# The last narrow piece of the light expert in one bank, and its next rows turned later

## What is computed

```python
def swiglu(x, w1, w3, w2):
    return (jax.nn.silu(x @ w1) * (x @ w3)) @ w2
```

## Time and profile before

| what | us |
|---|---|
| median of 3 runs (lowest to highest) | 1273.45 (1273.17 to 1274.38) |
| the profiled execution | 1273.87 |
| its span, first to last instruction | 1272.2 |
| PE busy | 1237.2 (97%) |
| DVE busy | 813.7 (64%) |
| ACT busy | 659.9 (52%) |
| mean granted PE clock | 0.992 |

### The profile page before, as it was taken

How to read it: one execution, slowest core, us unless ns; L and a number is a source line. 1 busy time by engine, 2 the same in 40 slices (tenths; PEclk the granted TensorE clock), 3 DMA queues, 4 the chain that set the end, 5 groups by cost and what they waited for, 6 DMA issues and landing times.

```text
span 1272.2 us, 15917 instructions
## 1 busy us (share of the span) xinstructions
PE 1237.2 (97%) x6263; PEld 935.3 (74%) x6263; DVE 813.7 (64%) x783; ACT 659.9 (52%) x683; POOL 87.3 (7%) x77
## 2 busy tenths in 40 slices
PE   9999999999999999999999989999979999799998
PEld 7878888888888888888776665566655666556886
DVE  6867756655456677689865655445554455555997
ACT  7577444444355674477754444434443444445774
POOL 0600001000004200020000000000000000000300
PEclk9999999999999999999999989999989999899999
DMA  9654549554545444479999999999999999999993
GB/s 376 275 198 135 177 167 371 193 199 167 197 154 210 174 158 166 166 275 404 351 362 420 421 380 382 403 407 421 421 369 380 423 420 422 383 384 423 420 421 148
DMA packets 56687, 391.91 MB, mean 308 GB/s; under 512 B 6720, under 2 KB 6720, under 8 KB 11584
## 3 DMA queue, kind: packets, MB, share of 16 engines
q1 hardware_dynamic: 53104, 374.84, 74.8%
q0 software_dynamic: 3360, 15.74, 3.2%
q10 hardware_dynamic: 144, 0.26, 0.1%
HBM read 384.78 MB, written 11.80 MB: 312 GB/s over the span
## 4 chain that ended last, share of the span: by engine, by line
PE 85%; DMA 5%; issue 4%; DVE 3%; ACT 1%; POOL 1%; SPq 1%; DVEq 0%; POOLq 0%; ACTq 0%
PE ps L574 23%; PE ps L575 21%; PE ps L576 21%; PE ps L1701 14%; DMA raw<-in_units 4%; PE ps L1245 3%; DVE wl L569 2%; DMA h<-in_x 1%; ACT wh L539 1%; POOL rst L712 1%; PE ps L1304 1%; DVE h L2323 0%; PE ps L1572 0%; PE ps L1618 0%; SPq L650 0%
## 5 line engine op out<-in xcount | busy, mean ns | idle before, releaser
L569 DVE TENSOR_TENSOR wl<-raw,wh 128x2048 fp32r<-128x2048 f32 x250 | 574.6, 2302 | 362.0 <-ACT wh L539 356.6
L539 ACT ACTIVATE wh<-raw 128x2048 fp32r<-128x2048 f32 x250 | 478.8, 1917 | 422.5 <-DMA raw<-in_units 262.8
L574 PE MATMUL ps<-wh,XT_h 128*128 128x512 f32 x944 | 379.9, 402 | 0.3 <-DVE wl L569 0.3
L575 PE MATMUL ps<-wl,XT_h 128*128 128x512 f32 x944 | 368.5, 390 | 0.0
L576 PE MATMUL ps<-wh,XT_l 128*128 128x512 f32 x944 | 368.5, 390 | 0.0
L574 PEld LDWEIGHTS ps<-wh,XT_h 128*128 128x128 f32 x944 | 177.3, 188 | 60.0 <-issue 23.5
L576 PEld LDWEIGHTS ps<-wh,XT_l 128*128 128x128 f32 x944 | 177.3, 188 | 37.9
L575 PEld LDWEIGHTS ps<-wl,XT_h 128*128 128x128 f32 x944 | 177.6, 188 | 33.1
L1701 PE MATMUL ps<-raw,few_X 128*64 128x256 f32 (+1 forms) x1152 | 133.5, 379 | 22.0 <-issue 20.1
L1701 PEld LDWEIGHTS ps<-raw,few_X 128*64 128x64 f32 x1152 | 79.0, 144 | 69.0 <-issue 39.2
L574 PE MATMUL ps<-wh,moe_gT_h 128*128 128x512 f32 x220 | 91.4, 415 | 0.2 <-DVE wl L557 0.2
(11 more groups left out here) (288 smaller groups left out, 1017.4 us busy)
## 6 DMA issues: line engine op xcount, KB each, us to landing
raw<-in_units SPq DMA_DIRECT2D x350, 1024.0 KB, 9.1
x_rows<-in_zeros POOLq DMA_DIRECT2D x8, 512.0 KB, 8.0
raw<-in_boot SPq DMA_DIRECT2D x5, 512.0 KB, 8.0
cols<-x_rows POOLq DMA_DIRECT2D x4, 512.0 KB, 9.2
y_rows<-xs POOLq DMA_DIRECT2D x4, 512.0 KB, 8.2
y_rows<-in_zeros POOLq DMA_DIRECT2D x6, 256.0 KB, 17.0
h<-in_x SPq DMA_DIRECT2D x1, 1024.0 KB, 13.0
rows<-in_rows SPq DMA_DIRECT2D x1, 896.0 KB, 16.9
```

What stands on the lines that cost most here:

```text
L539: nc.scalar.activation(wh[:, U.split_slot(j), :], raw[:, U.raw_slot(j), :], ACT.Copy).then_inc(hi_ready, 1)
L569: nc.vector.tensor_tensor(wl[:, s, :], raw[:, U.raw_slot(j), :], wh[:, s, :].bitcast(F32), ALU.subtract).then_inc(lo_ready, 1)
L574: nc.tensor.matmul(o, xh, bh, start=start, stop=False)
L575: nc.tensor.matmul(o, xh, bl, start=False, stop=False)
```

## The change

`few_places` gives the narrow piece two places in bank 2 (columns 0 to 127 for the gate product and 128 to 255 for the up product) and doesn't use bank 3. `few_gate_unit` computes both with one product per chunk and half, whose moving operand takes 128 columns of `w1` and 128 of `w3` (two runs, 256 columns apart). The wait for `g_ready` of the piece before is now only at k == 2, which the narrow piece doesn't have. The rows of p + 3 are turned after down step 6 and no longer after step 3, and in the expert in position 0 those of its second expert ahead of step 6 and no longer ahead of step 4. ACT copies them in steps 7 and 8.

```diff
         def few_places(p, s):
-            width = 256 if s < WIDE else 128
-            return ps[:, 2, 0:width], ps[:, 3, 0:width], width
+            if s < WIDE:
+                return ps[:, 2, 0:256], ps[:, 3, 0:256], 256
+            return ps[:, 2, 0:P], ps[:, 2, P:2 * P], P
...
-                    if u in (6, 7) and p + 3 < E:
-                        rows_hi(p + 3, u - 6)
+                    if u in (7, 8) and p + 3 < E:
+                        rows_hi(p + 3, u - 7)
...
-                    if u in (6, 7) and scatter is None:
-                        rows_hi(2, u - 6)
+                    if u in (7, 8) and scatter is None:
+                        rows_hi(2, u - 7)
...
-                    if u == 4 and scatter_at is None:
+                    if u == 6 and scatter_at is None:
                         rows_T(2)
...
-                if s > 0 and k == (2 if s < WIDE else 0):
+                if s > 0 and k == 2:
                     pe.wait_ge(g_ready, pieces_done(p, s - 1))
...
-                    for o, at in ((z1, 0), (z3, 256)) if s == WIDE else (((z1, z3)[k // 2], 0),):
-                        of = [w[:, a, at + half * width:at + (half + 1) * width] for half in range(2)]
-                        last = few_halves(o, few_X[:, c, :], of, c == 0, c == KC - 1)
+                    if s < WIDE:
+                        o, of = (z1, z3)[k // 2], [w[:, a, half * width:(half + 1) * width] for half in range(2)]
+                    else:
+                        o = ps[:, 2, 0:2 * P].rearrange("p (z n) -> p z n", z=2)
+                        by_matrix = w[:, a, :].rearrange("p (z h n) -> p z h n", z=2, h=2)
+                        of = [by_matrix[:, :, half] for half in range(2)]
+                    last = few_halves(o, few_X[:, c, :], of, c == 0, c == KC - 1)
...
-                    if u == 3 and p + 3 < E:
+                    if u == 6 and p + 3 < E:
                         rows_T(p + 3)
```

## The result

The changed kernel takes 1255.4 us in the median of 4 runs (1254.77 to 1259.13), beside 1273.74 for the kernel before on the same chip. The ratio is 0.9862, with a 95% interval of 0.9842 to 0.9882. The profiled execution took 1254.77 us, 19.1 less than the profiled one of before (forecast 21.1). The range held the median, and the forecast of 1252.3 was about 3 us too low.

A forecast was written before the change was run, and what follows sets the result against it. PE and transfers were taken as nearly even, with PE waiting for bank 3 and transfers then pausing. The gains 1.5 + 7.0 + 6.6 + 6.0 = 21.1 us gave a median of 1252.3 us, range 1247.5 to 1258.5.

The forecast's parts named there:

- The wait is for bank 3, behind a landing: Before light unit 20, PE waits for DVE's `few_up`, queued behind a landed unit's split; three waits, 20.1 us, go.
- The products themselves, 0: In the six narrow units, 16 longer products with a two-run operand take about 1.95 us per unit, gaining nothing.
- Earlier pairs gain what transfers gain, 7.0 and 6.6 us: In the first and second pair, unbroken transfers at 421 GB/s regain 7.0 and 6.6 us.
- rival A: In the down part, 384 GB/s is its own limit, so each pair gains only 3.0 us; 1263 us, chance 0.08.
- The new wait, 1.1 + 2.6 + 2.6: Before the turn in down step 0, PE waits for DVE's `lo`: 1.1, 2.6 and 2.6 us in the three pairs.
- the start of light unit 23: In the third pair, light unit 23 starts at 1115.14 from its own pair's gain, about 21 us earlier in all.
- the last pair's own gain: In the third pair, PE gains 6.0 us by light unit 23 and keeps it to the end.
- The expert in position 0, 1.5 us: In the expert in position 0, turning rows later removes 2.37 us of PE idle time; 1.5 us gained, between 0 and 2.4.
- The clock: At the new waits before down step 0's turn, 2.6 us lies nearer to 2.37 us, which kept the full clock.
- rival B: In down step 0, the new wait lowers the clock, costing about 4 us in all; 1256.5 us, chance 0.17.
- the expected sign of no stretch below 1 in the pairs: In the profile after, the granted clock has no window below 1 in the pairs.
- The turned rows in the pairs: In the pairs, turning rows after down step 6 removes two waits of about 2.5 us, with no separate gain counted.

The follow-up runs named there:

- e3: The changed kernel with the narrow piece's two products sharing bank 3 and unit 20 waiting for `few_up` of piece 4 as before; 1270.0 us, ratio 0.9964.
- e6: The kernel before with rows turned late and DVE's `up` and `few_up` of piece 4 ahead of the split of wide unit 21; 1254.87 us, ratio 0.9842.
- e2: The kernel before with only the turns of rows moved as in the change; 1269.39 us, ratio 0.9968.
- e4: The changed kernel with ACT's and DVE's narrow-piece work and piece 4's copies before the split of wide unit 23 in the pairs; 1253.36 us, ratio 0.9837.
- e8: The changed kernel with light units 3 to 20 of each pair loaded by half only, results not the reference's; 1242.12 us, ratio 0.9745.
- e7: The changed kernel with the turn in the expert in position 0 put back ahead of step 4; 1256.73 us, ratio 0.9855.
- a0: The changed kernel, unaltered, run again as reference for later experiments; 1256.45 us, ratio 0.9849.
- e1: The changed kernel with the turns of rows back at their old places, so the narrow piece's change alone; 1263.86 us, ratio 0.9913.
- e5: The changed kernel with light unit 20 computed twice in each pair, 1.95 us more PE work each; 1253.59 us, ratio 0.9830.

## Why the prediction was right, step by step

- *The wait is for bank 3, behind a landing:* right, shown by e3 (bank 3 kept, wait kept), e6 (bank 3 kept, `few_up` earlier) and the one named releaser in e2.
- *The products themselves, 0:* right, 1.95 us each in e3.
- *Earlier pairs gain what transfers gain, 7.0 and 6.6 us:* measured 61.69 - 54.67 = 7.0 and 61.23 - 54.62 = 6.6. The landing of wide unit 22 in the third pair agrees: it comes 15.1 us earlier, as 1.5 + 7.0 + 6.6 says. That transfers would stay near 421 GB/s through the down part was the doubtful step, and rival A is out.
- *The new wait, 1.1 + 2.6 + 2.6:* measured 0.54 + 2.80 + 3.09 = 6.4. Its cause was named rightly (e4, e8), and so was the start of light unit 23: 21.0 us earlier, beside 21.1 in the sum. Of these 15.1 were there at the landing of wide unit 22, so the last pair's own gain up to there is 5.9 (forecast 6.0).
- *The expert in position 0, 1.5 us:* the first pair begins at 646.32, where it began at 647.77, 1.45 less. By times at the end (e7) the term can't be confirmed.
- *The clock:* the mis-sized term. I took 2.6 us of wait to be nearer to 2.37 us, which had shown the full clock, and left the low clock to rival B with 0.17. It came in the first trace, where it costs 21.0 - 19.4 = 1.6 us, so the expected sign of no stretch below 1 in the pairs failed. It came after about half of such waits in the other traces (a0, e1, e6, e7), once even after 2.37 us. Where it is absent (e4, e5) the medians are 1253.4 and 1253.6, close to the forecast of 1252.3, though each of these kernels has another edit of its own. So forecast and rival B are both partly true: the mechanism of B, at about half its price (4 us). The last expert gives back another 0.3 us (106.84 us from light unit 32 to the end of the span, 106.56 before).
- *The turned rows in the pairs, "in the terms above already":* right for the sum, but it hid how much hangs on them. Left where they were, they would have made a second new wait of 2.9 us with a low clock in two pairs (e1), and taken back about 7 of the 18 us. The prediction should have priced the change without them.

## What to carry to other kernels

When PE and transfers are nearly even, price a removed wait by what the transfers regain (spacing of the splits that a landing released), and look for the next operation that stands in an in-order queue behind a landing: it becomes the new wait. An engine's wait for a bank can be cured by the bank or by the order of the reader's queue, and both gave the same time here. Where PE has time to spare, a wait of 2 to 3 us can cost more than the work that would fill it.

## What the runs showed of the hardware

The granted clock fell to 1.2 GHz (0.50 in 763 to 766 of a0) after idle times of PE as short as 2.11 us. The eleven traces have 19 idle times between 2.0 and 3.4 us. After nine of them the clock was low (2.11, 2.37, 2.45, 2.73, 2.77, 2.86, 2.94, 3.09 and 3.34 us) and after ten it was full (2.07, 2.18, 2.37 twice, 2.39, 2.53, 2.80, 2.83, 2.84 and 3.04). After the nine of 4.69 to 7.41 us it was always low, and after shorter ones never. So between 2 and 3.4 us the length of the wait doesn't decide it, and the same wait of 2.37 us came out both ways. The Trainium skill, TensorE: Matmul & The Clock Gate, section "HAM oscillation — how this bites in real kernels", has waits between bursts put the clock back to half. The traces agree for all the long waits and for about half of the short ones, with a unit of 1.94 us taking up to 3.63. The cost was 1.3 to 1.7 us of PE each time, and in the early pairs up to 2.5 us of transfer time behind it. A kernel with more work and no such wait (e5) was 2.9 us faster in the median.
